# Recurrence front of a hybrid transformer step: shorter VectorE masks, key products copied by ScalarE and masked by GpSimd

## What is computed

```python
def step(S, inp):
    r_t, w_t, k_t, v_t, kk_t, a_t = inp
    S = (S * w_t[:, :, None, :]
         - jnp.einsum('bhvk,bhk->bhv', S, kk_t)[..., None] * (kk_t * a_t)[:, :, None, :]
         + v_t[..., None] * k_t[:, :, None, :])
    return S, jnp.einsum('bhvk,bhk->bhv', S, r_t)
```

## Time and profile before

| what | value |
|---|---|
| median of 3 runs | 1872.31 us (1867.74 to 1872.33) |
| profiled execution, its own time | 1873.63 us |
| its span, first to last instruction | 1871.8 us |
| TensorE busy | 1754.2 us, 94% of the span |
| VectorE busy | 1083.1 us, 58% |
| ScalarE busy | 802.6 us, 43% |
| GpSimd busy | 364.5 us, 19% |
| mean granted TensorE clock | 0.99 |

### The profile page before, as it was taken

One profiled execution on the slowest core, in us unless ns is written; L12 is line 12 of the kernel. 1 busy time (PEld: TensorE's weight loads), 2 busy tenths in 40 slices (PEclk: granted clock), 3 DMA queues, 4 the chain that ended last, 5 costly groups with the idle time before them and its releaser, 6 DMA issues. The chain is left out here.

```text
span 1871.8 us, 46197 instructions
## 1 busy us (share of the span) xinstructions
PE 1754.2 (94%) x19693; PEld 1638.1 (88%) x19693; DVE 1083.1 (58%) x2356; ACT 802.6 (43%) x1723; POOL 364.5 (19%) x270
## 2 busy tenths in 40 slices
PE   7999878889999999999999998888899999999997
PEld 6998666678889999999989986767798999999997
DVE  4423967664296482747453348776627738466563
ACT  3423645552264252434443256454326525334352
POOL 3234200012311103020233440101142030201112
PEclk9999999999999999999999999999999999999999
DMA  9662600003432223132327343000021132222311
GB/s 338 197 155 93 182 5 3 3 7 91 138 107 86 78 74 107 52 96 74 96 77 213 102 140 91 6 2 7 25 68 46 60 98 79 85 77 76 94 55 57
DMA packets 215973, 161.11 MB, mean 86 GB/s; under 512 B 21968, under 2 KB 213146, under 8 KB 215770
## 3 DMA queue, kind: packets, MB, share of 16 engines
q1 hardware_dynamic: 213818, 156.13, 28.4%
q0 software_dynamic: 1952, 2.03, 0.3%
HBM read 154.99 MB, written 3.15 MB: 84 GB/s over the span
## 5 line engine op out<-in xcount | busy, mean ns | idle before, releaser
L2561 DVE SCALAR_TENSOR_TENSOR x<-PS,mod,x 128x320 f32<-128x320 f32 (+2 forms) x240 | 90.7, 433 | 295.2 <-PE PS L1048 295.2
L1083 PE MATMUL PS<-T_hi,wsplit 128*128 128x320 f32 x768 | 170.0, 309 | 0.0
L795 POOL TENSOR_TENSOR SfR<-ring,SfR 128x768 fp32r<-128x768 f32 (+1 forms) x24 | 41.2, 1717 | 581.9 <-ACT SfR L1720 581.9
L1047 PE MATMUL PS<-in_hi,win 128*128 128x320 f32 x480 | 150.6, 321 | 1.6 <-ACT mix L1770 0.9
L1048 PE MATMUL PS<-in_hi,win 128*128 128x320 f32 x480 | 144.9, 309 | 0.0
L1047 PE MATMUL PS<-hid_hi,wsplit 128*128 128x320 f32 x440 | 133.1, 310 | 0.0
L1048 PE MATMUL PS<-hid_hi,wsplit 128*128 128x320 f32 x440 | 132.5, 309 | 0.0
L1083 PEld LDWEIGHTS PS<-T_hi,wsplit 128*128 128x128 f32 x768 | 128.5, 188 | 0.0
L1083 PE MATMUL PS<-h_hi,wsplit 128*128 128x320 f32 x576 | 127.6, 309 | 0.0
L1083 PE MATMUL PS<-T_lo,wsplit 128*128 128x320 f32 x384 | 118.7, 309 | 0.0
L2016 ACT ACTIVATE wsplit<-Sf 128x512 fp32r<-128x512 f32 x96 | 59.8, 629 | 130.0 <-DVE Sf L2611 72.3
(11 more groups left out here) (518 smaller groups left out, 5433.4 us busy)
## 6 DMA issues: line engine op xcount, KB each, us to landing
ring<-in_w_ada SPq DMA_DIRECT2D x47, 1024.0 KB, 6.9
ring<-in_ffn_w_in SPq DMA_DIRECT2D x88, 512.0 KB, 5.1
ring<-in_ffn_w_out SPq DMA_DIRECT2D x16, 768.0 KB, 4.3
ring<-in_ffn_w_out SPq DMA_DIRECT2D x16, 640.0 KB, 4.0
ring<-in_w_in SPq DMA_DIRECT2D x7, 1024.0 KB, 10.0
ring<-in_w_in SPq DMA_DIRECT2D x10, 512.0 KB, 5.5
ring<-in_w_in SPq DMA_DIRECT2D x16, 256.0 KB, 5.9
ring<-in_w_out SPq DMA_DIRECT2D x16, 256.0 KB, 6.5
```

Source lines behind the costliest of these rows:

```text
L795: nc.gpsimd.tensor_tensor(lo, raw_w, hi, SUB).then_inc(wl_ready(), 1)
L1047: mm(lat[:, 0:TH], w, v[:, 0:TH], start=(n == 0), stop=(n == total - 1))
L1083: last = mm(bank[:, 0:TH], (w_lo if p == 1 else w_hi)[:, k, :], (v_lo if p == 2 else v_hi)[:, k, :], start=(q in (A11, A12, S1_) and k == ...
L2561: last = V.scalar_tensor_tensor(x[:, m, a:b], bank[:, at:at + b - a], mod[:, gate_at + m, s:s + 1], x[:, m, a:b], MUL, ADD)
```

## The change

VectorE no longer masks the four products of a pair in one instruction. It multiplies the BA product and the A-with-B product by two near masks (`NEAR`, 256 elements: the masked BA goes to a place of its own, `DT`, beside `D1`), and then A with B by the far mask (`FAR`, 128 elements). ScalarE copies the products KA, KR and BR unmasked to `LP` (`keys_copy`, 384 elements), after `FAR` of the pair. GpSimd masks KA there (128 elements) and then KR and BR (256 elements). TensorE's `squares` wait for ScalarE's copy, since they write over the columns that it reads; the KA product of round three waits for GpSimd's first mask, the last products of the group for its second. The products of B are written in the order R, A instead of A, R, for which the moving operand's rows are read in reverse.

In ScalarE's order, `keys_copy(0)` comes behind the token copies (and the row splits), then `keys_copy(n)` and the left copy of pair n-1 by turns. In the third round ScalarE copies both results in one instruction (256 elements), without a wait for VectorE, whose copy L2438 is gone. The signals `right_ps` and `right_sb` count five rounds instead of six. VectorE's job behind round three is now behind round four's right copies. The mask tables are reordered to match.

```diff
+        NEAR = pure_and_unit(1920)
+        FAR, DT, D1 = heads(1280), heads(1920), heads(2048)
+        W1_AND_Y = [mix[:, b + 640:b + 640 + 2048].rearrange("p (a s) -> p a s", a=2)[:, :, 0:128] for b in pb]
...
                     for n, (p, ht, d, t) in enumerate(GROUPS[g]):
-                        e.wait_ge(lp_sb.sem, lp_sb.upto(l, 4 * g + n + 1))
-                        nc.gpsimd.tensor_tensor(E1D[p], LP[p][:, :, BA, :],
+                        e.wait_ge(near_sb.sem, near_sb.upto(l, 4 * g + n + 1))
+                        nc.gpsimd.tensor_tensor(E1D[p], DT[p],
                                                 eye64[:, :].unsqueeze(1).to_broadcast([128, 2, 64]), ADD).then_inc(
                                                     diag_sb(), 1)
+                    for n, (p, ht, d, t) in enumerate(GROUPS[g]):
+                        e.wait_ge(raw_sb.sem, raw_sb.upto(l, 4 * g + n + 1))
+                        nc.gpsimd.tensor_tensor(LP[p][:, :, KA, :], LP[p][:, :, KA, :],
+                                                masks[:, d, 0:64].unsqueeze(1).to_broadcast([128, 2, 64]),
+                                                MUL).then_inc(lp_sb(), 1)
+                    for n, (p, ht, d, t) in enumerate(GROUPS[g]):
+                        out_ = LP[p][:, :, KR:BR + 1, :].rearrange("p h a t -> p h (a t)")
+                        nc.gpsimd.tensor_tensor(out_, out_, masks[:, d, 64:192].unsqueeze(1).to_broadcast([128, 2, 128]),
+                                                MUL).then_inc(out_sb(), 1)
...
-                            mm(ps[2 * p + hd][cs, 128:256], H[hs, B_ + d, c], H[hs, d:d + 3:2, c], start=True, stop=True)
+                            mm(ps[2 * p + hd][cs, 128:256], H[hs, B_ + d, c], by_r_and_a(H, hs, d, c), start=True, stop=True)
...
+                    def by_r_and_a(H, hs, d, c):
+                        return H[hs, 0:4, c].rearrange("p (a d) t -> p a d t", a=2)[:, ::-1, d, :]
...
                     def squares(g, n):
 
                         p = GROUPS[g][n][0]
-                        e.wait_ge(near_sb.sem, near_sb.upto(l, 4 * g + n + 1))
+                        e.wait_ge(raw_sb.sem, raw_sb.upto(l, 4 * g + n + 1))
                         for hd, ck, cs, os in halves:
-                            last = mm(ps[2 * p + 1][cs, 64 * hd:64 * hd + 64], LP[p][cs, hd, BA, :], D1[p][cs, hd, :],
+                            last = mm(ps[2 * p + 1][cs, 64 * hd:64 * hd + 64], DT[p][cs, hd, :], D1[p][cs, hd, :],
...
+                            for n, p, there in two_:
+                                e.wait_ge(lp_sb.sem, lp_sb.upto(l, base + n + 1))
...
+                            e.wait_ge(out_sb.sem, out_sb.upto(l, base + n + 1))
...
+                        def keys_copy(n):
+                            p = group[n][0]
+                            e.wait_ge(far_sb.sem, far_sb.upto(l, base + n + 1))
+                            act(LP[p][:, :, 0:3, :].rearrange("p h a t -> p h (a t)"), PS[:, 2 * p:2 * p + 2, 0:192],
+                                ACT.Copy).then_inc(raw_sb(), 1)
+
                         def left_copy(rnd, n):
...
+                            if rnd == 3:
+                                act(W1_AND_Y[p], PS[:, 2 * p:2 * p + 2, 0:128], ACT.Copy).then_inc(left_sb(), 1)
...
-                        for rnd in range(1, 7):
+                        keys_copy(0)
+                        for n in range(1, ng):
+                            keys_copy(n)
+                            left_copy(1, n - 1)
+                        left_copy(1, ng - 1)
+                        for rnd in range(2, 7):
                             for n in range(ng):
                                 left_copy(rnd, n)
...
+                        def far_part(n):
+                            p, ht, d, t = group[n]
+                            V.tensor_tensor(FAR[p], PS[:, 2 * p:2 * p + 2, 256:320],
+                                            masks[:, d, 192:256].unsqueeze(1).to_broadcast([128, 2, 64]),
+                                            MUL).then_inc(far_sb(), 1)
+
                         def factors(n):
...
-                            V.tensor_tensor(LP[p].rearrange("p h a t -> p h (a t)"), two[:, :, 0:256],
-                                            masks[:, d, :].unsqueeze(1).to_broadcast([128, 2, 256]),
-                                            MUL).then_inc(lp_sb(), 1)
-                            V.tensor_tensor(FAR_NEAR[p], two[:, :, 256:320].unsqueeze(1).to_broadcast([128, 2, 2, 64]),
+                            V.tensor_tensor(NEAR[p], two[:, :, 192:320].rearrange("p h (a t) -> p a h t", a=2),
                                             near[:, d, 0:2, :].unsqueeze(2).to_broadcast([128, 2, 2, 64]),
                                             MUL).then_inc(near_sb(), 1)
...
-                            else:
-                                V.tensor_copy(Y_[p], got).then_inc(right_sb(), 1)
 
                         for n in range(ng):
                             factors(n)
-                        for rnd in range(1, 7):
+                            far_part(n)
+                        for n in range(ng):
+                            right_copy(1, n)
+                        for n in range(ng):
+                            right_copy(2, n)
+                        for rnd in range(4, 7):
                             for n in range(ng):
                                 right_copy(rnd, n)
-                            if rnd != 3:
+                            if rnd != 4:
                                 continue
```

More of the change, by code:

```diff
@@ L412, in pure_and_unit @@
             return [mix[:, b + at:b + at + 256].rearrange("p (a h t) -> p a h t", a=2, h=2) for b in pb]
[L414 to L418, removed]
+        NEAR = pure_and_unit(1920)
+        FAR, DT, D1 = heads(1280), heads(1920), heads(2048)
+        W1_AND_Y = [mix[:, b + 640:b + 640 + 2048].rearrange("p (a s) -> p a s", a=2)[:, :, 0:128] for b in pb]
+        E1D, D2T, D4I, W_, Y_ = heads(512), heads(640), heads(2048), heads(1536), heads(1664)
         D2 = pure_and_unit(1408)
@@ L426, in build @@
         tA, tK, tB, tV = range(4)
-        KA, KR, BA, BR = range(4)
+        KA, KR, BR = range(3)
         def a_w1_and_far(p, r, hd):
@@ L433, in b_and_br @@
         def b_and_br(p, r, hd):
-            at, step = pb[p] + 256 + 64 * hd, 704 + 192 * hd
+            at, step = pb[p] + 256 + 64 * hd, 640 + 192 * hd
             return mix[r, at:at + 2 * step].rearrange("p (a t) -> p a t", t=step)[:, :, 0:64]
@@ L537, in build @@
         prod_ps, lp_sb, diag_sb, near_sb = (sig(x_, n2) for x_ in ("prod_ps", "lp_sb", "diag_sb", "near_sb"))
+        far_sb, raw_sb, out_sb = (sig(x_, n2) for x_ in ("far_sb", "raw_sb", "out_sb"))
         left_ps, left_sb = sig("left_ps", 6 * n2), sig("left_sb", 6 * n2)
-        right_ps, right_sb = sig("right_ps", 6 * n2), sig("right_sb", 6 * n2)
+        right_ps, right_sb = sig("right_ps", 5 * n2), sig("right_sb", 5 * n2)
         ug_ps, ug_sb = sig("ug_ps", n2), sig("ug_sb", n2)
@@ L1361, in squares @@
                         for hd, ck, cs, os in halves:
-                            last = mm(ps[2 * p][cs, 64 * hd:64 * hd + 64], D1[p][cs, hd, :], LP[p][cs, hd, BA, :],
+                            last = mm(ps[2 * p][cs, 64 * hd:64 * hd + 64], D1[p][cs, hd, :], DT[p][cs, hd, :],
                                       start=True, stop=True)
@@ L1429, in recurrence @@
                                     hd, far, own_, c = sides(there, i)
-                                    last = mm(ps[2 * p + 1][own_, c], D4I[p][far, hd, :], W_[p][far, hd, :],
-                                              start=True, stop=True)
-                                    if i == 3:
-                                        last.then_inc(right_ps(), 1)
+                                    mm(ps[2 * p + 1][own_, c], D4I[p][far, hd, :], W_[p][far, hd, :],
+                                       start=True, stop=True)
+                            for n, p, there in two_:
+                                e.wait_ge(lp_sb.sem, lp_sb.upto(l, base + n + 1))
                             for i in range(4):
@@ L2432, in right_copy @@
                                                 ADD).then_inc(right_sb(), 1)
[L2433 removed]
+                            else:
                                 V.tensor_tensor((D4I if rnd == 2 else N4I)[p], got,
@@ L2730, in tables @@
     m = np.zeros((128, 2, 4, CH), np.float32)
-    m[:, 0, 0], m[:, 0, 1], m[:, 0, 2], m[:, 0, 3] = i < t, i <= t, same & (i < t), i <= t
-    m[:, 1, 0], m[:, 1, 1], m[:, 1, 2], m[:, 1, 3] = i > t, i >= t, same & (i > t), i >= t
+    m[:, 0, 0], m[:, 0, 1], m[:, 0, 2], m[:, 0, 3] = i < t, i <= t, i <= t, ~same & (i > t)
+    m[:, 1, 0], m[:, 1, 1], m[:, 1, 2], m[:, 1, 3] = i > t, i >= t, i >= t, ~same & (i < t)
     out["t_masks"] = m.reshape(128, 2, 4 * CH)
     nf = np.zeros((128, 2, 4, CH), np.float32)
-    nf[:, 0, 0], nf[:, 0, 1] = ~same & (i > t), same & (i > t)
```

(3 more changed lines are left out.)

11 lines of the change are left out of this document (6 added, 5 removed).

## The result

The changed kernel took 1889.8 us (median of 4 runs, 1886.0 to 1892.3) against 1871.5 for the kernel before (four runs; the table above has three of them): a ratio of 1.0091, 95% interval 1.0072 to 1.0111, slower by 18.3 us. In a later set, beside 29 runs of the kernel before, it stood 16.7 us over (experiment 9). The forecast was +10 (1882.3 us), the range 1873 to 1890. The profiled execution was the lowest of the four, 1886.0 us with a span of 1884.2, which is 12.4 over the profiled execution of before.

What follows compares the result with a forecast made beforehand. The prediction took TensorE's waits for copies in ten group fronts as the bound, VectorE's queue up to the first right copy. Fronts summed to 11.0 us, less 1 for stops: net +10, 1882.3 us, range 1873 to 1890.

Steps and rivals of the forecast that it cites:

- VectorE's masks shorter: Front's start: a pair's masks cost 0.54 us instead of 0.94; up to the first left copy 0.57 us won.
- ScalarE's new order: Round one: key copies 2 and 3 queue behind left copies, so round two's second half comes 0.75 us later.
- this sign: Plain groups (0, 2, 5, 7): prediction wrong if round four comes less than 0.5 us late; 0.77 forecast.
- Group 1 and the row splits: Fronts outside the plain groups: +1.0 us each in groups 1, 6, 3 and 8, +2.3 each in 4 and 9.
- Third round: One wide ScalarE copy replaces two narrow ones: first half 0.22 us later, of which 0.05 shows.
- The moved job: VectorE's job, moved to before round five's right copies, holds copies by less: 0.15 us a group come back.
- GpSimd: 0: GpSimd's key and output masks cost 0, covered by rounds two to six; wide masks estimated at 0.70 us.
- I take 1 us: TensorE's "issue" stops, mostly behind the front: later arrival may shorten them, 1 us subtracted of 18.6 us.
- rival (a): TensorE's issue stops swallow the loss: half gives 1878, all 1872, nearly all stops gone 1865; chance 0.21.
- Added waits on TensorE: eight a group, for signals long raised: 0: Waits added to TensorE's stream in each group, for signals already raised, cost 0.
- rival (b): TensorE's longer waits, most in groups 4 and 9, lower its granted clock: +5 us, 1887; chance 0.12.
- Rival (c): VectorE alone sets the front, key copies 2 and 3 not awaited: -2 us, 1870; chance 0.04.

Runs made afterwards that it cites:

- experiment 9: The changed kernel measured again beside 29 runs of the kernel before: 1888.6 us, ratio to before 1.0097.
- Experiment 10: The kernel before, with TensorE issuing products(3) ahead of squares(0) and nothing else: 1872.8 us, ratio to before 1.0008.
- experiment 8: The changed kernel with key copies first, row splits early, and products(3) ahead of squares(0) on TensorE: 1868.9 us, ratio to before 0.9975.
- Experiment 1: The changed kernel with ScalarE's four key copies ahead of all left copies of round one: 1876.2 us, ratio to before 1.0024.
- Experiment 2: The changed kernel with the row splits of groups 3, 4, 8 and 9 moved to the ends of the groups ahead: 1884.9 us, ratio to before 1.0066.
- experiment 5: The kernel before with only the third round's one wide ScalarE copy; VectorE's job keeps its place: 1872.9 us, ratio to before 1.0001.
- experiment 6: The kernel before with the third round's one wide ScalarE copy and the moved VectorE job: 1874.0 us, ratio to before 1.0013.
- experiment 4: The changed kernel with key copies first and row splits early, each GpSimd mask done twice: 1875.3 us, ratio to before 1.0009.
- (7): The changed kernel with key copies first and row splits early, but third round and VectorE's job as before: 1874.9 us, ratio to before 1.0010.
- 11: The changed kernel with keys first, splits early, products(3) ahead of squares(0), and FAR's mask on GpSimd too: 1868.3 us, ratio to before 0.9983.
- (3): The changed kernel with key copies ahead of left copies and row splits moved early, both together: 1872.7 us, ratio to before 1.0010.

## Why the prediction was right, and where it was off

**VectorE's masks shorter: right.** From the first mask of group 0: squares(0) at 1.20 (forecast 1.28), NEAR(3) 2.52 (2.6), first right copy 3.06 (3.1), first left copy 3.56 (3.65). Experiment 10 shows that this was the bound; experiment 8, that the gain is real once nothing stands in its way.

**ScalarE's new order: right, and the cause of most of the loss.** Squares(2) at 4.28 (4.39), squares(3) at 4.83 (4.95), round two's second half at 6.27 (6.40); before it was 5.65, so 0.62 later where 0.75 was forecast. All steps came about 0.1 us early, most of it at the first handover: VectorE to ScalarE took 0.04 (251.87 to 251.91) where 0.10 was forecast. Experiment 1 undid the order: -13.6 us, for the 10 to 11 that follow from the forecast's terms. Round four then came 0.54 late in all four plain groups, not 0.77; the forecast called itself wrong below 0.5, so this sign was passed narrowly.

**Group 1 and the row splits: right.** TensorE's timelines, counted from the end of products(0), give round two's second half 1.2 us later in group 1 (1.15 in the forecast's chain), 1.1 in group 3 (1.15), and 2.23 and 2.45 in groups 4 and 9 (2.45). Over the ten groups it is 11.8 us later, where the forecast's figures for that point come to 12.5. Experiment 2 undid the splits: -3.5 us in the fronts for 3.4, and -3.1 to -4.9 in time.

**Third round: right to be near nothing** (experiment 5). **The moved job: the 1.5 us credited to it did not show** in the time (experiment 6). **GpSimd: 0, right by experiment 4**; the price of 0.70 for the wide mask was 0.64. But in three combinations (4, 7 and 11) GpSimd's later end met VectorE's row. In the changed kernel itself it did not: its rows of this kind have a mean of 817 ns.

**The term with the wrong sign is the last one, "I take 1 us" for the stops.** It was to be subtracted, since a later arrival might let TensorE's instructions catch up. The waits table of after has these as its largest stops put down to "issue" (us, times, longest), against the earlier trace rows:

```profile
PE PS L1535 <- issue: 4.2, 4, 1.3
PE PS L1530 <- issue: 3.8, 3, 1.7
PE PS L1532 <- issue: 3.6, 3, 1.4
```

These are three of the five lines of the chunk's transition. The same three in the kernel before (L1518 is L1532 after, L1521 is L1535, L1516 is L1530):

```profile
PE PS L1518 <- issue: 4.0, 4, 1.1
...
PE PS L1521 <- issue: 1.4, 1, 1.4
...
PE PS L1516 <- issue: 1.2, 2, 0.6
```

Over the whole kernel such stops sum to 23.2 us before, to 26.9 after and to 25.3 in the second profile of the changed kernel: they grew by 2 to 4 us instead of shrinking by 1. So rival (a) fell, and the signal named for it (shrinking by over 3 us) did not come. In the ten groups alone they went from 18.7 to 22.2 and 20.8.

Nearly all of the growth is in the transition's five lines, and it comes with the new masks, not with the late front. The stops there sum to 8.0 to 9.2 us in all four profiles of kernels with the old masks (before, (5), (6), (10)), and to 13.5 to 16.0 us in all ten with the new ones, whatever their order and whether their fronts are late or early. (7) and (6) place them with the masks' part of the change, not with the third round or the moved job. From the start of "U and G" to their ends the ten groups take 99.8 us on average in the four profiles and 104.3 in the ten, so some 5 us of cost lie behind the front. The forecast had nothing there but "Added waits on TensorE: eight a group, for signals long raised: 0". The waits are written ahead of the first of the five lines, and most of the stops fall at later ones. Whether it is these waits, or the new places of the moved products in SBUF, no run tells apart; that stays open. It also shows why (3) is level: over the ten groups its round four starts 3.4 us earlier than before, and these stops are 4.8 us more.

Elsewhere the stops are no fixed property of a place. TensorE's timeline in group 2, the changed kernel's first profile:

```profile
354.16 0.46 PE L1460 MATMUL PS<-mix 64*64 64x64 f32 x15
355.78 0.27 PE L1460 MATMUL PS<-mix 64*64 64x64 f32 x1 [1.16 <-issue]
```

and the second profile of the same kernel, where the set runs through:

```profile
353.18 0.58 PE L1460 MATMUL PS<-mix 64*64 64x64 f32 x16
```

Up to that set the two executions agree within 0.02 us in this group; then one stands still for 1.16 us between the 15th and the 16th matmul of a set.

**The size.** In the profiled executions the sum held. Added up over the ten groups, each from the end of its products(0) to its own end, the changed kernel is 11.1 us slower in its first profile and 10.6 in its second, stops included, where the forecast has +10; the whole executions differ by 12.4 and 11.0. The medians differ by 18.3 and 16.7. Of the 7.5 us between the forecast 1882.3 and the median 1889.8, 2.4 lie in the profiled execution (1886.0 for 1883.6) and 5.1 in the step from there to the median: the forecast took 1.3 off, since the profiled execution of before lay that far above its median, while the profiled executions of the changed kernel were the lowest of theirs both times, 3.8 and 4.0 below. Part of this goes with the clock: the profiled execution of before had a mean granted clock of 0.990, those of the changed kernel 0.992 and 0.993. At the 1.3 us for 0.001 that the last section reads from the runs of before, my estimate is that at one clock the profiled executions would differ by some 15 us. The 2 to 3 us that are left stay open: executions without a profile show no lines.

**Where luck helped.** The mechanism was right, the median's place in the range was not earned. The range reached up to 1890 for rival (b), which did not come, and 1889.8 lies 0.2 us inside it.

**Rival (b), the clock, did not come**: the granted clock is 1.00 over all ten fronts in both profiles of the changed kernel, and its mean over the runs is 0.991 and 0.992 for the changed kernel against 0.992 for before. **Rival (c)** would have needed an order that the change did not have; experiment 1 is that order, with the row splits in place, and lands 4.9 us over before, not 2 under.

## What to carry to other kernels

When work leaves the engine that bounds a stage, write down the new order of every engine's queue before counting the gain: here 24 us of VectorE's work went, and two positions in ScalarE's queue cost some 17 us. Undoing them only made the kernel level; it took a new order on TensorE too to gain 4 us, and GpSimd's third mask with a row moved out of its way to gain 7. A copy that starts a chain goes ahead of copies that end one, and side jobs that lay in an engine's idle time must move when that idle time becomes the path. Once a bound moves, try again the orders that made no difference under the old one (experiments 8 and 10 are one edit with two outcomes), and ask what stands behind the added work on each queue, not only when its result is wanted. Then look behind the stage that was changed: here the fronts of (3) became shorter and TensorE's stops behind them longer.

## What the runs showed that I had not expected

- **VectorE and GpSimd exclude each other for whole instructions** when VectorE's has two inputs in SBUF: 0.82 us became 2.72 and 2.09, each time ending 0.68 us after GpSimd's; a mask of 0.64 us on GpSimd became 1.94. The kernel before has it too: at 61.11 a 128-wide VectorE instruction with two inputs in SBUF, 0.34 us in most of its 18 executions, took 2.49. These rows begin while the other engine is still at work, so such a row looks like slow work and not like a wait.
- **TensorE's stops without a releaser come and go between executions of one kernel**: 1.16 us within a set of matmuls in one profile, none there in the other. Over a whole kernel they summed to 18.6 to 32.9 us in the fourteen profiles.
- **The spread of the runs follows the granted clock.** The 29 runs of before in the last set go from 1865.3 to 1879.3 us, with mean granted clocks of 0.995 down to 0.986; time and clock have a correlation of -0.89, about 1.3 us for 0.001; the runs do not say which of the two drives the other. A difference of 5 us between two single executions is therefore no finding.
